# Attention's last quad, the router's chain, the final norm and the matmul engine's feed-forward tails reordered, on one core

## What is computed

```python
def swiglu_ffn(x, w_up, w_down):
    gate, up = jnp.split(x @ w_up, 2, axis=-1)
    return (jax.nn.silu(gate) * up) @ w_down          # D_FF = 2816, x: (256, 1024)

x = _layer_norm(ALPHA * x + dilated_attention(x, w_in, w_out, rel_bias), gain, bias)
x = _layer_norm(ALPHA * x + swiglu_ffn(x, w_up, w_down), gain, bias)
...
x = x + gt1 * (fourier_mix(modulate(rmsnorm(x, g_mix), sh1, sc1)) @ w_fourier)
h = modulate(rmsnorm(x, g_ffn), sh2, sc2)
logits = h @ w_router + b_router
top_val, top_idx = lax.top_k(logits, 2)
top_w = jax.nn.softmax(top_val, axis=-1)
for e in range(8):                                     # expert width 3584
    out = out + gate[..., e:e + 1] * swiglu(h, w1[e], w3[e], w2[e])
x = x + gt2 * out
return rmsnorm(x, final_g)
```

## Time and profile before

| | |
|---|---|
| median of 3 runs | 2565.1 us |
| lowest and highest | 2560.89, 2566.06 us |
| the profiled execution | 2565.6 us |
| its span, first to last instruction | 2563.8 us |
| PE busy | 2482.5 us, 97% |
| DVE busy | 1902.3 us, 74% |
| ACT busy | 1450.1 us, 57% |
| mean granted TensorE clock | 0.970 |
| read from memory | 630.72 MB, 246 GB/s over the span |

### The profile page before, as it was taken

One profiled execution on the slowest core, in us unless ns is written; L12 is line 12 of the kernel. 1 busy time (PEld: TensorE's weight loads), 2 busy tenths in 40 slices (PEclk: granted clock), 3 DMA queues, 4 the chain that ended last, 5 costly groups with the idle time before them and its releaser, 6 DMA issues.

```text
span 2563.8 us, 35862 instructions
## 1 busy us (share of the span) xinstructions
PE 2482.5 (97%) x13052; PEld 2106.8 (82%) x13052; DVE 1902.3 (74%) x2252; ACT 1450.1 (57%) x1712; POOL 91.3 (4%) x141
## 2 busy tenths in 40 slices
PE   8998999999989999999899989999999999999996
PEld 8787888999977788888788878888888888888885
DVE  6657875555567667365698458999898989898897
ACT  4454343444434444343444337787777777878785
POOL 0000000000001000010110000000000000000000
PEclk9999998999989999998899989999999999999998
DMA  7456765665647754453798348999999999999994
GB/s 248 153 183 236 256 231 156 177 146 150 155 125 264 267 189 105 94 71 48 261 365 313 115 148 307 353 353 352 351 349 357 348 356 352 352 354 351 346 358 186
DMA packets 288975, 633.23 MB, mean 247 GB/s; under 512 B 10826, under 2 KB 72309, under 8 KB 288560
## 3 DMA queue, kind: packets, MB, share of 16 engines
q1 hardware_dynamic: 268368, 556.83, 61.7%
q0 software_dynamic: 20512, 75.07, 11.8%
HBM read 630.72 MB, written 1.14 MB: 246 GB/s over the span
## 4 chain that ended last, share of the span: by engine, by line
PE 49%; issue 45%; DVE 3%; DMA 1%; ACT 1%; POOL 0%; SPq 0%; DVEq 0%; POOLq 0%; ACTq 0%
PE ps L707 14%; PE ps L708 14%; PE ps L709 13%; DMA gate_rows<-mod 1%; PE ps L731 1%; PE ps L1292 1%; PE ps L1182 1%; PE ps L1341 1%; PE ps L1063 1%; PE ps L1048 1%; PE ps L1325 1%; PE ps L1338 1%; PE ps L1068 1%; PE ps L1304 1%; PE ps L814 0%
## 5 line engine op out<-in xcount | busy, mean ns | idle before, releaser
L2051 DVE TENSOR_TENSOR w_lo<-raw,w_hi 128x1024 fp32r<-128x1024 f32 x722 | 875.1, 1224 | 512.7 <-ACT w_hi L1553 488.2
L1553 ACT ACTIVATE w_hi<-raw 128x1024 fp32r<-128x1024 f32 x722 | 756.1, 1059 | 721.4 <-PE ps L709 712.6
L707 PE MATMUL ps<-w_hi,x_hi 128*128 128x512 f32 (+1 forms) x1936 | 750.2, 387 | 15.3 <-DVE h_lo L2269 7.1
L709 PE MATMUL ps<-w_hi,x_lo 128*128 128x512 f32 (+1 forms) x1936 | 732.9, 379 | 0.0
L708 PE MATMUL ps<-w_lo,x_hi 128*128 128x512 f32 (+1 forms) x1936 | 732.8, 379 | 0.0
L707 PEld LDWEIGHTS ps<-w_hi,x_hi 128*128 128x128 f32 x1936 | 371.3, 192 | 97.7 <-issue 23.9
L709 PEld LDWEIGHTS ps<-w_hi,x_lo 128*128 128x128 f32 x1936 | 370.9, 192 | 67.6
L708 PEld LDWEIGHTS ps<-w_lo,x_hi 128*128 128x128 f32 x1936 | 371.9, 192 | 62.3 <-issue 1.0
L2051 DVE TENSOR_TENSOR w_lo<-big,w_hi 128x1024 fp32r<-128x1024 f32 x336 | 404.5, 1223 | 21.2 <-ACT w_hi L1553 0.5
L1553 ACT ACTIVATE w_hi<-big 128x1024 fp32r<-128x1024 f32 x336 | 357.9, 1065 | 94.6 <-PE ps L709 94.4
L707 PE MATMUL ps<-w_hi,h_hi 128*128 128x512 f32 x760 | 297.5, 391 | 1.2
(11 more groups left out here) (369 smaller groups left out, 2193.3 us busy)
## 6 DMA issues: line engine op xcount, KB each, us to landing
raw<-in_moe_w SPq DMA_DIRECT2D x170, 1024.0 KB, 5.1
big<-in_moe_w SPq DMA_DIRECT2D x168, 1024.0 KB, 5.2
big<-in_w_ada POOLq DMA_DIRECT2D x48, 1024.0 KB, 7.3
raw<-in_ffn_w_up SPq DMA_DIRECT2D x44, 1024.0 KB, 5.2
raw<-in_attn_w_in SPq DMA_DIRECT2D x36, 1024.0 KB, 5.0
raw<-in_ffn_w SPq DMA_DIRECT2D x33, 1024.0 KB, 7.2
raw<-in_ret_w_in SPq DMA_DIRECT2D x24, 1024.0 KB, 5.2
raw<-in_ffn_w_down SPq DMA_DIRECT2D x22, 1024.0 KB, 4.9
```

What stands on the lines that cost most here:

```text
L707: mm(dst, lhs[0], rhs[0], start=start, stop=False)
L709: return mm(dst, lhs[1], rhs[0], start=False, stop=stop)
L1553: nc.scalar.activation(w_hi[:, m % SPLIT, :], raw(SLOT_OF[b])[:, h * HALF:(h + 1) * HALF], ACT.Copy).then_inc(hi_ready, 1)
L2051: V.tensor_tensor(w_lo[:, m % SPLIT, :], raw(SLOT_OF[b])[:, h * HALF:(h + 1) * HALF], w_hi[:, m % SPLIT, :].bitcast(F32), ALU.subtract).th ...
```

## The change

On PE: `turn(units - 1)` of an odd tail moves between the two token tiles of the gate block. The `Fori` loops of `ffn2` and `moe` are written out. In front of the transposes of the seams x1, x3 and m1 it issues 5 + 4, 5 + 4 and 9 + 0 products of constants (`ident` by four constant squares, plain fp32, 512 columns) into a bank that nobody reads, and around the transposes of m3 5 and 3 products of zeros (the fast form). `quad_out(2, ...)` moves one head later, and `quad_turn(3)` stands in the middle of its last half. `token_rows(1, ...)` moves behind the triangular products. The last `scatter` signals each token tile.

On ACT and DVE: the splits of quads 1 and 2 move ahead of the next head's maxima and exponentials, `quad_low(0)` ahead of `quad_scale`, and the weight split `ahead("att_in", 35)` behind them at head 12. `hidden` of unit 0 moves ahead of the unit's last weight split. Constants and zero tiles are made between the Fourier stage's weight splits instead of in the router's chain, and the split `ahead("fourier", 3)` moves behind the rank computation. ACT copies half of the first expert's x_lo. Inside each item the weighting moves ahead of the last half of the weight split. The final norm is written out tile by tile, with one fused operation for root and `final_g`, a last store in two halves, and `final_g` loaded early into a place of its own.

The diff, cut to its core (`sp` now stores row tile 0 and two halves of row tile 1):

```diff
 ACT_STAGE = {"m1": 0, "m3": 1}
-QUAD_BANK = (6, 7, 6, 6)
+WARM = {"x1": (5, 4), "x3": (5, 4), "m1": (9, 0)}
+QUAD_BANK = (6, 7, 6, 5)
 Z_BANK = (5, 6, 7, 5, 7, 7)
...
-  pool.wait_ge(x_summed.sem, x_summed.after("moe", 1))
-  pool.dma_start(ln_gb[:, 0, :], a["final_g_2"].partition_broadcast(P)).then_inc(ln_in, 16)
+  pool.dma_start(final_g, a["final_g_2"].partition_broadcast(P)).then_inc(aux["final_g"], 16)
...
+  def keep_warm(stage, n):
+
+      for _ in range(n):
+          mm(ps[:, 6 if stage == "x1" else 7, :], ident, sq[:, 0:4, :].rearrange("p m n -> p (m n)"), start=True, stop=True)
+
+  def zero_products(n):
+
+      for _ in range(n):
+          mm(ps[:, 7, :], m_zero[:, 0:P], m_zero, start=True, stop=True)
...
+          if stage in WARM:
+              if stage == "x3":
+                  pe.wait_ge(part_added, 6)
+              keep_warm(stage, WARM[stage][t])
...
-      if between:
-          for u in range(2, units):
-              unit(u, 6 * u - 2, at)
-              downs(u - 1, 6 * u + 2, False, False, at)
-      else:
-          with pe.Fori(0, units - 2) as i:
-              here = At(i, at.e)
-              unit(2, 10, here)
-              downs(1, 14, False, False, here)
+      for u in range(2, units):
+          unit(u, 6 * u - 2, at)
+          downs(u - 1, 6 * u + 2, False, False, at)
...
           for t in range(tiles):
               for k in range(KD):
                   last = mm3(ps[:, 4 + t, 0:T], lhs(k, t), column_tile(w, k, slice(0, T)), k == 0, k == KD - 1)
+              if t == 0:
+                  turn(units - 1, at)
           last.then_inc(split_free, 2)
-          turn(units - 1, at)
           up_free(units, at)
...
-      else:
-          pe.wait_ge(part_added, 6)
...
+          if between and k == 0:
+              between()
...
-      elif h > 12:
+      elif h in (13, 14):
           quad_out(h - 13, 1)
+      elif h == 15:
+          quad_out(2, 0)
       att_mix(h, 0)
       att_mix(h, 1)
       for n in blocks[1:]:
           att_block(n)
       if h == 11:
           quad_turn(0)
-      elif 12 <= h < 15:
+      elif h in (12, 13):
           quad_out(h - 12, 0)
-  quad_turn(3)
+  quad_out(2, 1, between=lambda: quad_turn(3))
   pe.wait_ge(fm_saved.sem, fm_saved.after("att", 3))
   wait_acc("att_out")
   accumulate_last("att_out", 3, x_tile, 6, start=True)
...
   modulation(3, "ffn2")
-
+  pe.wait_ge(yc_ready, 1)
+  zero_products(5)
   modulated_input("m3")
+  zero_products(3)
...
   token_rows(0, x_hi, 1, 4)
-  token_rows(1, x_lo, 0, 2)
   pe.wait_ge(ranked, 1)
   m0, m1 = route[:, 0, 1, :], route[:, 1, 1, :]
   mm(ps[:, 4, 0:8], tri, m0, start=True, stop=True)
@@ -1463,7 +1480,7 @@
...
-  token_rows(1, x_lo, 2, 4)
+  token_rows(1, x_lo)
...
+          if stop:
+              last.then_inc(rows_summed, 1)
+      if not stop:
+          last.then_inc(scattered, 1)
...
           ahead(stage, n, at)
-          ahead(stage, n + 1, at)
+          ahead(stage, n + 1, at, (0,))
+          in_last()
+          ahead(stage, n + 1, at, (1,))
...
-      ahead("att_in", n)
+      if n < 35:
+          ahead("att_in", n)
...
+      if h == 12:
+          quad_high(1)
+          quad_high(2)
       if h + 1 < AH:
           att_exp(h + 1, 0)
           att_exp(h + 1, 1)
@@ -1781,11 +1807,11 @@
       if h == 11:
           quad_high(0)
       elif h == 12:
-          quad_high(1)
-          quad_high(2)
-      elif h > 12:
+          ahead("att_in", 35)
+      elif h in (13, 14):
           ahead("att_out", h - 13)
   quad_high(3)
+  ahead("att_out", 2)
   root("ln2")
...
+  act.wait_ge(gathered, 2)
   act.wait_ge(m_g_saved, 1)
-  nc.scalar.activation(stat[:, 28:29], ones[:, 0:1], ACT.Silu).then_inc(m_x_high, 1)
+  nc.scalar.activation(x_lo[:, 4:8, 0:P], ps[:, 7, :].rearrange("p (k s) -> p k s", k=4), ACT.Copy
+                       ).then_inc(m_x_high, 1)
+  nc.scalar.activation(stat[:, 28:29], ones[:, 0:1], ACT.Silu)
...
       glu("moe", 7, False, 1, at, per_item=7, after_turn=lambda: keep(0, e + 2), in_second=next_low,
-          before_last=next_high)
...
+          before_last=next_high, in_last=weighted_high)
+
+  nc.scalar.activation(stat[:, 26:27], ones[:, 0:1], ACT.Sqrt)
+  for t in range(TT):
+      act.wait_ge(x_summed.sem, x_summed.after("moe", t))
+      square(x_tok, t, work[:, t, :])
+      act.wait_ge(moments.sem, moments.after("fin", t))
+      nc.scalar.activation(stat[:, 20 + t:21 + t], stat[:, 16 + t:17 + t], ACT.Sqrt).then_inc(roots.sem, 1)
...
           for b in range(4):
+              if (u, b) == (0, 3):
+                  hidden(u, n + 3, at)
               block(n + b, at)
               if u and b == 0:
                   low(u - 1, at)
               if (u, b) == (0, 1) and in_first:
                   in_first()
-          hidden(u, n + 3, at)
           if u:
+              hidden(u, n + 3, at)
               block(n + 4, at)
               block(n + 5, at)
...
           block(n, at)
-          block(n + 1, at)
+          ahead(stage, n + 1, at, (0,))
+          in_last()
+          ahead(stage, n + 1, at, (1,))
...
+      if h == 12:
+          quad_low(1)
+          quad_low(2)
       if h + 1 < AH:
           att_max(h + 1, 0)
           att_max(h + 1, 1)
       for n in blocks[:1]:
           att_low(n)
-      if h == 12:
-          quad_low(1)
-          quad_low(2)
-      elif h > 12:
+      if h in (13, 14):
           quad_add(h - 13, 1)
+      elif h == 15:
+          quad_add(2, 0)
       att_save(h, 0)
       att_save(h, 1)
       for n in blocks[1:]:
           att_low(n)
+      if h == 11:
+          quad_low(0)
       if h % 4 == 3:
           quad_scale(h // 4)
-      if h == 11:
-          quad_low(0)
-      elif h > 12:
+      if h == 12:
+          ahead("att_in", 35)
+      elif h in (13, 14):
           ahead("att_out", h - 13)
-      if 12 <= h < 15:
+      if h in (12, 13):
           quad_add(h - 12, 0)
   quad_low(3)
+  quad_add(2, 1)
+  ahead("att_out", 2, halves=(0,))
   layer_norm("att_out", "x3", 2, used("att_out", 3), 1.0)
+  ahead("att_out", 2, halves=(1,))
   save_fm("x3", 4)
   ahead("att_out", 3)
...
-  for b in range(3):
-      ahead("fourier", b)
-  dve.wait_ge(router_cut, 1)
-  V.tensor_tensor(router_cols[:, :, EXPERTS:], router_w[:, :, :],
-                  router_cols[:, :, 0:EXPERTS].bitcast(F32), ALU.subtract).then_inc(router_cut, 1)
-  residual("fourier", "fourier", used("fourier", 3), 2)
-  save_modulation(3, 5)
-  modulate("m3", x_tok, 3, 0, x_hi, x_lo)
-  ahead("fourier", 3)
-
-
+  ahead("fourier", 0)
...
   link(V.tensor_copy(table_f[:, 0:EXPERTS], iota[:, 0:EXPERTS]))
+  ahead("fourier", 1)
+  for half in range(2):
+      c = slice(half * BANK, half * BANK + BANK)
+      V.tensor_copy(m_yc_hi[:, c], m_none)
+      V.tensor_copy(m_yc_lo[:, c], m_none)
+  V.tensor_copy(m_selt[:, :], m_none[:, 0:T]).then_inc(sel_kept, 1)
+  ahead("fourier", 2)
+  dve.wait_ge(router_cut, 1)
+  V.tensor_tensor(router_cols[:, :, EXPERTS:], router_w[:, :, :],
+                  router_cols[:, :, 0:EXPERTS].bitcast(F32), ALU.subtract).then_inc(router_cut, 1)
+  residual("fourier", "fourier", used("fourier", 3), 2)
+  save_modulation(3, 5)
+  modulate("m3", x_tok, 3, 0, x_hi, x_lo)
...
+  ahead("fourier", 3)
...
   dve.wait_ge(gathered, 2)
-  V.tensor_copy(x_lo[:, :, 0:P], psf[:, 6 * BANK:8 * BANK].rearrange("p (k s) -> p k s", k=KD)).then_inc(m_x_cut, 1)
+  V.tensor_copy(x_lo[:, 0:4, 0:P], ps[:, 6, :].rearrange("p (k s) -> p k s", k=4)).then_inc(m_x_cut, 1)
...
-  for half in range(2):
-      c = slice(half * BANK, half * BANK + BANK)
-      V.tensor_copy(m_yc_hi[:, c], m_none)
-      V.tensor_copy(m_yc_lo[:, c], m_none)
-  V.tensor_copy(m_selt[:, :], m_none[:, 0:T]).then_inc(sel_kept, 1)
...
+      def weighted_low():
+
+          dve.wait_ge(yc_high, e + 1)
+          V.scalar_tensor_tensor(m_yc_lo[:, :], ps[:, 0:2, :].rearrange("p b n -> p (b n)"), m_gate,
+                                 m_yc_hi[:, :].bitcast(F32), ALU.mult, ALU.subtract).then_inc(yc_ready, 1)
...
+  def weighted_rows(t):
+
+      dve.wait_ge(rows_summed, t + 1)
       for half in range(2):
           c = slice(half * BANK, half * BANK + BANK)
...
+  dve.wait_ge(aux["final_g"], 16)
+  weighted_rows(0)
+  summed_rows(0)
+  weighted_rows(1)
+  mean_square(0)
+  summed_rows(1)
   dve.wait_ge(x_summed.sem, x_summed.after("moe", 1))
-  dve.wait_ge(ln_in, 32 * 8 + 16)
-  rms_moments("fin")
-  rms_scale("fin", x_tok, work)
+  scaled_rows(0, 1)
+  mean_square(1)
+  scaled_rows(1, 2)
```

More of the change, by code:

```diff
@@ L1543, in link, with ahead @@
                 act.wait_ge(act_step, steps[0])
-            def ahead(stage, n, at=HERE):
+            def ahead(stage, n, at=HERE, halves=(0, 1)):
                 b = FIRST_BLOCK[stage] + n + AHEAD
@@ L1549, in ahead @@
                             at.plus(LANDING[b], 32 if b < FIRST_BLOCK["moe"] else 16, 112))
-                for h in range(2):
+                for h in halves:
                     m = 2 * (b) + h
```

59 lines of the change are left out of this document (35 added, 24 removed).

## The result

| | before | after |
|---|---|---|
| median | 2565.6 us | 2522.3 us (4 runs, 2520.5 to 2525.3) |
| profiled execution, span | 2565.6, 2563.8 | 2521.8, 2520.0 |
| PE busy | 2482.5 us | 2478.1 us |
| mean granted clock | 0.970 | 0.987 |

The ratio on record is 0.9843, with a 95% interval of 0.9826 to 0.9861: 1.6% faster. (The two medians alone give 0.9831.

The account below looks back on a forecast made before the run. PE, busy 97% of the span, was taken to set the time through idle and half-clock stretches. Terms 12.1 + 1.8 + 10.75 + 2.5 + 7.3 + 1.0 + 0 + 6.5 = 42 off 2565.6 gave 2523 us; range 2511 to 2541.

Parts of the forecast that it names:

- Odd tails, 12.1: Odd tails of ffn0, ffn1, ffn2: three waits, 7.1 us, go, and half clock behind them, 5.0 us; sum 12.1.
- Unit 0's hidden, 1.8: ffn0 and ffn2: PE's two waits for DVE's product with unit 0's gate go, 1.8 us in all.
- Attention's end, 10.75: End of attention: 6.65 us of idle PE and 5.0 us of half clock go, less 0.9: 10.75 us.
- through the heads, short waits never cost the clock: Attention's heads: argument that short waits leave the clock up, used against the rival that the clock isn't held, chance 0.13.
- Constants' products, 2.5: Seams x1, x3, m1: products of constants in front gain 0.6, 0 and 1.9 us; sum 2.5, upper bound 6.4.
- the sign of being wrong: Windows at clock 0.50 behind x1, x3, m1 or in the expert stage's first 6 us would show the forecast wrong.
- The lower bound: Seams x1, x3, m1: clock falls despite the products, which take twice as long, 5 us later at each, -15.
- Router, 7.3: Router's chain to the experts' start: earlier logits' copy, no m_selt wait, full clock; 7.3 us, bounds 4.3 and 8.2.
- Loops 1.0: PE's loops written out: nothing in ffn2, 1.0 us in the expert stage, bounds 0 and 4.
- weighting 0: Expert items: weighting ahead of the last half weight split costs 0, margin 0.4 us; if it fails, 4 in all.
- end 6.5: End of the program: earlier weighting and final sum 1.3 us, final norm and early final_g 5.2; sum 6.5.
- The slow rival: Expert loop no longer stays in PE's instruction store: 40 packets fetched anew at 2.4 us, 96 us, 2619; chance 0.05.

Follow-up runs that it names:

- the combined kernel: Kernel after with 6 and 2 constant products at x1, 7 and 0 at m1, unit 0's low half earlier in ffn0 and ffn2: 2516.3 us, ratio 0.9825.
- the second execution: The kernel after, unchanged, executed once more beside two variants on one chip: median 2523.9 us, ratio 0.9854.
- tails and router alone: Two kernels, each before with one edit: odd tails' turn moved, 2553.5 us; router's chain reordered without products of zeros, 2556.9 us.

## Why the prediction was right, point by point

**Odd tails, 12.1.** Measured 4.1 + 3.4 + 4.3 = 11.8 in after, 12 alone. What was late next was named wrongly in part: not ACT's weight split but h_lo itself, which in ffn1 stands behind a filter step on DVE and still costs 0.5 us.

**Unit 0's hidden, 1.8.** The step that failed. "The split that it pushes back by 1.2 us is wanted a whole block later" is true, but PE's next need of DVE is not that split. It is `h_lo` of unit 0, which must be made before unit 1's up products may start, and on DVE it stands behind two splits and two modulation steps that take 2.67 us together (DVE's timeline of after; the combined kernel makes h_lo ahead of the modulation steps). The last line is PE's wait:

```profile
253.31 1.22 DVE L2088 TENSOR_TENSOR w_lo<-raw,w_hi 128x1024 fp32r<-128x1024 f32 x1
254.44 2.67 DVE L2217 SCALAR_TENSOR_TENSOR big<-big,silu_c 128x1024 f32<-128x1024 f32 x2
257.03 1.22 DVE L2306 TENSOR_TENSOR h_lo<-ps,h_hi 128x1024 fp32r<-128x1024 f32 x1
...
258.30 0.50 PE L712 MATMUL ps<-w_hi,x_hi 128*128 128x512 f32 x1 [0.51 <-DVE h_lo L2306]
```

Each wait gave 0.3, some 0.6 in all, for the 1.8 forecast. An error of the size of 1 us, and the one that pointed to a better kernel.

**Attention's end, 10.75.** PE's last output product comes 12.9 us earlier: 17.9 ahead (766.4 against 748.6) against 5.0 before. PE's idle time is 0.7 us, as "under 2" had it. The sum left out a term: I priced half clock in two windows of pure products, 5.3 and 4.7 us, but the first stretch had begun earlier, and PE was busy for 3.8 us between its waits, at 0.50 too. That is 1.9 us, and with it the sum is 12.65. It also answers my "through the heads, short waits never cost the clock": here they stood beside it. The row of before that I didn't read:

```profile
715.90:720.80 4.90, 3.83 (x20) 3.70 (x19) 3.32 (x8) 2.71 (x6) 1.65 (x2) 0.50 0.58 164
```

What was late next further on I hadn't looked for: the filter in ffn1, 1.1 us, so that attention's end and x3 together gave 11.8.

**Constants' products, 2.5.** x1: 1.3 us later, and 18 products instead of 10 in 4 us, 2.0: 0.7 for 0.6. x3: from product to product 12.7 us instead of 11.4, so 1.3 later, and 2.9 us at half clock gone, 1.45: next to nothing, as forecast. m1: ffn2 starts 0.95 us later for the 1.05 forecast. But behind it the sign of being wrong came in after's first execution, 3.4 us at 0.50 from 1232.3 on, and the stage got 0.8 with unit 0's 0.3 in it instead of 2.8. In the second execution that stretch was missing and the stage 1.6 us shorter, near the forecast. Without the products the clock was at 1.00 behind m1 in one execution and at 0.50 in before, so that the products hold it there isn't shown. The lower bound, that they run at half clock and cost 5 us a seam, didn't come.

**Router, 7.3.** Measured 8.4 in after, 7.7 alone and without zeros, each against the longest chain of before. What I wanted the products of zeros for, the clock at the experts' start, is there without them in two kernels. Yet the chain takes 31.8 to 32.5 us in the eight traces with them and 33.3 and 36.2 in the two without. I charged them 0.8; they seem to have given something instead. No run leaves out only them, so what they are worth stays open.

**Loops 1.0, weighting 0, end 6.5.** Measured 1.1 (loops put back), no wait for w_lo at an item's first blocks, and 7.2. At the end the scatter and the sum gave 1.3 for 1.3. Behind the last sum DVE needed 3.4 us (2514.04 to 2517.49) for 3.4; against the 8.8 of before that is 5.4, and the 5.2 in my sum was a slip. The last 0.6 lie behind DVE: the span ends 2.5 us after its last instruction instead of 3.1. That fits the smaller last store, which I had left out. (The new end takes 21.7 us from the table's last border in all nine traces that have it; the old one 29.0 in before's kept trace, the shortest, and 29.4 to 30.4 in the four others.)

**The slow rival's price was wrong.** I put 2.4 us on each of 40 packets, 96 us. Where fetches do come, the 12 packets of a pass together cost 1.2 us. Had the body been too long, seven jumps would have cost 8.4 us at that price, and the kernel would have been at 2531, still faster.

**What the sum had no term for.** Stages that the change leaves alone gave +1.0, -1.6, +0.5 and +2.3, and the Fourier stage, where it only adds DVE's constants and products in a wait, -0.8: together +1.4. The -1.6 is one stretch at half clock of 6.8 us instead of 3.4; for the others I take the same cause, without having shown it. That the total is right to 1 us is luck in two ways. These terms cancel, as do the errors of the stages (attention and router more than forecast, unit 0 and m1 less). And the forecast's starting point is an execution of before 3.7 us longer than its later medians: from those the sum of 42 would have led to 2520, while the medians of one round are only 38.5 us apart. The same starting point is a reason why tails and router alone move the medians by 8 and 5 us where their traces show 12 and 8 in their own stages. Where the half clock falls in later stages is another; that is argued from the two executions of one kernel, not shown for each case.

## What to carry to other kernels

Price a wait on the matmul engine with the half clock behind it and around it: windows with the granted clock give that price in one row, also where short waits and work alternate. When you move an operation forward on a vector engine, look for the next thing that the matmul engine needs from that same engine; it is often the next link of the same chain. Filler products in front of a stage pay when they end as the data arrives: count them from the length of the wait, and expect the next chain (here the filter) to take part of what is won. And take the starting point from several executions: a single trace can lie some us beside the median, as much as a whole part of the change is worth.

## What the runs showed that I had not expected

PE falls to half clock though it is busy all the time, in rows of one-column products and once among attention's heads (720.8 to 724.2, busy 3.40 of 3.40 us at 0.50). Four wide products among 48 of one column didn't prevent it. Where it falls changes between two executions of one kernel. A loop body of some 2500 instructions on PE (products and weight loads) comes with 12 packets a pass and 1.2 us of standing still a jump, one of 1260 with no packets behind the first pass and no wait.
